# Attention in a hybrid decoder step: logits of two units in a row, DVE's transposition work behind the next maximum, page products on POOL

## The reference

```python
s = jnp.einsum('bqhd,bkhd->bhqk', q_blk, k_all)          # 16 heads of 64
s = s + fq_blk.transpose(0, 2, 1)[..., None] - f_k[:, :, None, :]
s = jnp.where((kpos[None, :] <= qpos[:, None])[None, None], s, -jnp.inf)
p = jax.nn.softmax(s, axis=-1)
return jnp.einsum('bhqk,bkhd->bqhd', p, v_all)
```

## Time and profile before

| what | value |
| --- | --- |
| median of 3 runs | 3183.25 us (3177.59 to 3183.7) |
| the profiled execution | 3182.08 us, of which the span is 3180.5 us |
| busy over the whole span | PE 2896.3 us (91%), DVE 1533.9, ACT 951.6, POOL 751.7 |
| attention phase, roughly 2012 to 2912 us | 28% of the span |
| one middle step of attention (steps 1 to 6; starts of unit 0 at 2160.18, 2267.46, 2374.71, 2481.99, 2590.73, 2697.97 and 2805.26 us) | 107.25 us (one is 108.74) |
| the first step, the last step up to PE's last sum | 110.4 us; 2805.26 to 2904.12 us |

### The profile page before, as it was taken

One profiled execution on the slowest core, in us unless ns is written; L12 is line 12 of the kernel. 1 busy time (PEld: TensorE's weight loads), 2 busy tenths in 40 slices (PEclk: granted clock), 3 DMA queues, 4 the chain that ended last, 5 costly groups with the idle time before them and its releaser, 6 DMA issues. The chain is left out here.

```text
span 3180.5 us, 41505 instructions
## 1 busy us (share of the span) xinstructions
PE 2896.3 (91%) x15730; PEld 2010.4 (63%) x15730; DVE 1533.9 (48%) x3562; ACT 951.6 (30%) x1547; POOL 751.7 (24%) x428
## 2 busy tenths in 40 slices
PE   6589999997899987999969999699999999995998
PEld 2367777776677875777857788344444444442767
DVE  1542222211877637531175115667766776663343
ACT  0322212211655544210042111143434334433000
POOL 1220000000000003000020000376677677676000
PEclk7689999998899998999989999699999999997999
DMA  9532222213466524221142331423322331313764
GB/s 335 186 90 80 54 86 80 77 47 118 158 227 199 160 90 179 82 74 48 47 178 73 77 47 52 127 71 104 104 54 82 104 94 45 101 32 122 249 206 127
DMA packets 281926, 355.19 MB, mean 112 GB/s; under 512 B 40044, under 2 KB 172460, under 8 KB 281681
## 3 DMA queue, kind: packets, MB, share of 16 engines
q1 hardware_dynamic: 279364, 344.23, 34.3%
q0 software_dynamic: 2304, 8.39, 0.7%
q10 hardware_dynamic: 72, 0.07, 0.0%
HBM read 250.28 MB, written 102.10 MB: 111 GB/s over the span
## 5 line engine op out<-in xcount | busy, mean ns | idle before, releaser
L2315 POOL TENSOR_TENSOR at_p_sum<-at_p_sum,at_p 128x1024 f32<-128x1024 f32 (+3 forms) x264 | 543.0, 2057 | 93.2 <-ACT at_p L2171 76.0
L2171 ACT ACTIVATE at_p<-psum 128x1024 f32<-128x1024 f32 (+1 forms) x320 | 286.6, 896 | 504.1 <-PE psum L2011 498.9
L2217 DVE CUSTOM_DVE_ANT_0 psum<-psum,at_f_wide 128x512 f32<-128x512 f32 (+3 forms) x640 | 376.8, 631 | 0.0
L2091 PE MATMUL psum<-at_p,at_v 128*64 128x512 f32 (+3 forms) x1280 | 305.4, 556 | 0.1
L672 POOL TENSOR_TENSOR kv_h_lo<-kv_aux,kv_h_hi 128x512 fp32r<-128x512 f32 x16 | 24.1, 1505 | 1060.2 <-ACT kv_h_hi L649 1023.4
L768 PE MATMUL psum<-kv_w_hi,kv_h_hi 128*128 128x512 f32 x512 | 201.5, 394 | 12.2 <-DVE kv_w_lo L964 12.2
L768 PE MATMUL psum<-gla_w_hi,gla_h_hi 128*128 128x512 f32 x512 | 201.3, 393 | 2.7 <-DVE gla_w_lo L964 2.7
L769 PE MATMUL psum<-kv_w_lo,kv_h_hi 128*128 128x512 f32 x512 | 200.5, 392 | 0.0
L770 PE MATMUL psum<-kv_w_hi,kv_h_lo 128*128 128x512 f32 x512 | 200.2, 391 | 0.0
L769 PE MATMUL psum<-gla_w_lo,gla_h_hi 128*128 128x512 f32 x512 | 199.5, 390 | 0.0
L770 PE MATMUL psum<-gla_w_hi,gla_h_lo 128*128 128x512 f32 x512 | 199.3, 389 | 0.0
(11 more groups left out here) (425 smaller groups left out, 6093.6 us busy)
## 6 DMA issues: line engine op xcount, KB each, us to landing
mod_w<-in_ada_w SPq DMA_DIRECT2D x12, 2048.0 KB, 17.9
at_f_wide<-F SPq DMA_DIRECT2D x32, 512.0 KB, 5.7
at_page<-in_cache_k SPq DMA_DIRECT2D x32, 512.0 KB, 3.9
gla_w_raw<-in_gla_w_in SPq DMA_DIRECT2D x6, 2048.0 KB, 7.8
mod_w<-in_kv_ada_w SPq DMA_DIRECT2D x4, 2048.0 KB, 9.9
v_gla<-gla_stage SPq DMA_DIRECT2D x32, 256.0 KB, 2.0
sg_gla<-gla_stage SPq DMA_DIRECT2D x32, 256.0 KB, 2.0
gl_sg<-sg_gla SPq DMA_DIRECT2D x16, 512.0 KB, 3.9
```

The lines of the kernel that those rows point to most:

```text
L2091: mm = pe.matmul(bank_o[half[a], skip:NB], v[u][:, i, half[a]], p_tile[e % PT][:, a, skip:NB], start=(i == 0), stop=(i == R * G + R - 1), ...
L2171: act.activation(p_tile[e % PT][:, :, skip:NB], pair_of(bank_st[e % 2])[:, :, skip:NB], ACT.Exp)\
L2217: op = dve.tensor_tensor_reduce(pair_of(at(n))[:, a, 0:w], pair_of(at(n))[:, a, 0:w], f_wide[:, a, c * NB:c * NB + w], 1.0, -3.0e38, ALU.s ...
L2315: pool.tensor_tensor(p_sum[s][:, :, skip:NB], p_sum[s][:, :, skip:NB], p_tile[e % PT][:, :, skip:NB], ALU.add).then_inc(p_added, 1)
```

## The change

Five edits, all in the attention phase:

1. PE takes two units together (`two_units`). It waits once for both pairs of banks, makes the masks of both, the maximum of slot e, the logits of e and of e + 1, the maximum of slot e + 1, the turn operation of e, the weighing of units e - 2 and e - 1, and the turn operation of e + 1. ACT does both exponentials first, then the turn work and the copy of `bank_o`.
2. On DVE (`some`), a turn operation of an odd slot comes behind the next slot's maximum; that of an even slot behind the maximum of the slot after it.
3. The slot behind unit 39 is gone. Its m_row is now `CARRIED` into slot 0 of the next step, and the last two weighings of a step lie in unit 0 and 1 of the next.
4. The product of page and query row runs on POOL (`weigh_page`), at the slots 1, 10, 20 and 31, behind that slot's addition. On DVE only the sums remain, each in two halves of 8 heads, at the slots 5, 7, 12, 14, 27, 29, 36 and 38.
5. SP waits for two more maxima before it loads the next V, and loads pages at the new slots.

```diff
-    page_at = (1, 5, 10, 12, 20, 29, 33, 38)
+    page_at = (1, 10, 20, 31)
+    score_at = (5, 7, 12, 14, 27, 29, 36, 38)
...
-                        sp.wait_ge(max_full, UN * (2 * j + u) + AHEAD + 1)
+                        sp.wait_ge(max_full, UN * (2 * j + u) + AHEAD + 3)
...
-                    pe.wait_ge(p_ready, UN * h + e + 1)
+                    pe.wait_ge(p_ready, UN * h + e + 2)
...
+                def two_units(j, u, e):
+
+                    logits_wait(j, u, e)
+                    for s in (e, e + 1):
+                        G, i = exp_units[s]
                         if i >= R * G:
-                            masks(bank_st[e % 2], (i - R * G) * P, g.hide_kq)
...
+                            masks(bank_st[s % 2], (i - R * G) * P, g.hide_kq)
+                    max_unit(j, u, e)
+                    logits(j, u, e)
+                    logits(j, u, e + 1)
+                    max_unit(j, u, e + 1)
+                    turn_unit(j, u, e)
                     if e:
+                        weigh_v(j, u, e - 2)
                         weigh_v(j, u, e - 1)
+                    elif not is_first(j, u):
+                        weigh_v(*previous(j, u), UN - 2)
+                        weigh_v(*previous(j, u), UN - 1)
+                    turn_unit(j, u, e + 1)
...
+                    for e in range(0, UN, 2):
+                        some(e, MAXIMA)
+                        if e:
+                            some(e - 1, TURNS)
+                        some(e + 1, MAXIMA)
+                        some(e, TURNS)
+                        for s in (e, e + 1):
+                            if s in score_at:
+                                score_page(j, u, score_at.index(s))
...
+                    pool.tensor_tensor(page[w % 2][:, :], page[w % 2][:, :], q_sample[u][:, :], ALU.mult).then_inc(page_prod, 1)
...
                     for e in range(UN):
                         add(j, u, e)
+                        if e in page_at:
+                            weigh_page(j, u, page_at.index(e))
```

More of the change, by code:

```diff
@@ L1762, in attention_phase @@
     max_slots = list(enumerate([(OWN, f) for f in last_maxima] + [(NEXT, f) for f in ahead]))
-    turn_slots = {2: (LAST, "sum", 3, 0), 3: (LAST, "pick", 3, 0), 4: (LAST, "spread", 3, 0),
+    turn_slots = {0: (CARRIED, "m_row", 2, 0), 2: (LAST, "sum", 3, 0), 3: (LAST, "pick", 3, 0), 4: (LAST, "spread", 3, 0),
                   6: (OWN, "sum", 0, 0), 7: (OWN, "pick", 0, 0), 8: (OWN, "spread", 0, 0),
@@ L1768, in attention_phase @@
                   26: (OWN, "sum", 2, 0), 27: (OWN, "pick", 2, 0), 28: (OWN, "spread", 2, 0), 30: (NEXT, "m_row", 1, 0),
-                  32: (NEXT, "turn", 3, 0), 35: (NEXT, "turn", 3, 1), UN: (NEXT, "m_row", 2, 0)}
+                  32: (NEXT, "turn", 3, 0), 35: (NEXT, "turn", 3, 1)}
     def slots_with(*whose):
-        slots, n_turn = [[] for _ in range(UN + 1)], 0
+        slots, n_turn = [[] for _ in range(UN)], 0
         for e, (who, (kind, a, b)) in max_slots:
@@ L1778, in slots_with @@
                     slots[e].append((who, "m_max", a // R, 0, 0))
-        for e in range(UN + 1):
+        for e in range(UN):
             if e in turn_slots and turn_slots[e][0] in whose:
@@ L1793, in attention_phase @@
     start_slots, AT_START = slots_with(OWN, NEXT)
-    mid_slots, EACH = slots_with(LAST, OWN, NEXT)
-    end_slots, _ = slots_with(LAST, OWN)
+    mid_slots, EACH = slots_with(LAST, CARRIED, OWN, NEXT)
+    end_slots, _ = slots_with(LAST, CARRIED, OWN)
     tail_slots = [(LAST,) + f[1:4] + (n,) for n, f in enumerate(f for f in turn_slots.values() if f[0] == LAST)]
     AT_END = sum(f[1] in ("sum", "pick", "spread", "m_row") for slot in end_slots for f in slot)
-    page_at = (1, 5, 10, 12, 20, 29, 33, 38)
+    MAXIMA, TURNS = ("max", "m_max"), ("turn", "m_row", "sum", "pick", "spread")
+    assert UN - 1 not in turn_slots
+    page_at = (1, 10, 20, 31)
+    score_at = (5, 7, 12, 14, 27, 29, 36, 38)
     f_slots = (R, 2 * R, 3 * R, 4 * R)
@@ L2149, in _ @@
                 run_steps(step)
+                weigh_v(PAIRS // 2 - 1, 1, UN - 2)
+                weigh_v(PAIRS // 2 - 1, 1, UN - 1)
                 for who, kind, a, b, n in tail_slots:
@@ L2181, in step @@
                 def step(j, u):
-                    for e in range(UN + 1):
-                        if e < UN:
-                            exponential(j, u, e)
+                    for e in range(0, UN, 2):
+                        exponential(j, u, e)
+                        exponential(j, u, e + 1)
                         for who, kind, a, b, n in slots_of(j, u)[e]:
                             filler(*whose(who, j, u), before(j, u), kind, a, b, n)
-                        for G in range(NG):
+                        if e == 0 and not is_first(j, u):
+                            copy_o(*previous(j, u), NG - 1)
+                        for G in range(NG - 1):
                             if units_to(G) == e:
                                 copy_o(j, u, G)
+                        for who, kind, a, b, n in slots_of(j, u)[e + 1]:
+                            filler(*whose(who, j, u), before(j, u), kind, a, b, n)
                 act.sem_inc(p_ready, 2)
@@ L2270, in step, with some @@
                 def step(j, u):
-                    for e in range(UN + 1):
-                        for who, kind, a, b, n in slots_of(j, u)[e]:
-                            turn_op(*whose(who, j, u), before(j, u), kind, a, b, n)
-                        if e in page_at:
-                            score_page(j, u, page_at.index(e))
+                    def some(s, kinds):
+                        for who, kind, a, b, n in slots_of(j, u)[s]:
+                            if kind in kinds:
+                                turn_op(*whose(who, j, u), before(j, u), kind, a, b, n)
+                    for e in range(0, UN, 2):
+                        some(e, MAXIMA)
[6 more added lines that the diff above has]
+                                score_page(j, u, score_at.index(s))
                 dve.sem_inc(turn_used, 1)
```

63 lines of the change are left out of this document (28 added, 35 removed).

## The result

The changed kernel takes **3129.27 us** (median of 4 runs, 3128.80 to 3129.90) where the kernel before takes 3181.42 (4 runs, 3177.59 to 3183.70): a ratio of 0.984, 95% interval 0.9829 to 0.9852, 52 us less. I had said 3155 us with a range from 3134 to 3176. The profiled execution has a span of 3128.0 us against 3180.5.

What follows compares the result with a forecast made beforehand. PE was taken to bound attention. Saving 4.4 - 0.9 = 3.5 us a middle step gave 24.5 over seven steps, plus 1.8 (first) and 0.5 (last): 26.8 off 3182.1, so 3155 us, range 3134 to 3176.

Steps and rivals of the forecast that it cites:

- the saving of a middle step: Attention's middle steps: 4.4 us saved on changes between kinds of PE products, less 0.9 us of added waits, 3.5 us.
- the three signs: Against the forecast: PE idle before plain pairs' second maximum, PE waiting for exponentials at many pairs, exponential waiting for POOL in group 3.
- The first weighing of two: PE's first of two weighings in a row takes 0.91 us, between bounds of 0.853 and 1.01.
- Turn operations: On PE they keep their price: four transposes some 0.55 us on either side of a weighing.
- Masked second maxima: Ten slots' maxima with a mask now stand behind logits: changes of kind return, 0.2 us each, 2.0 us a step lost.
- The waits: PE waiting for DVE in the new order, mainly at four short pairs: 5.3 us a step, 0.9 more than before.
- Turns behind: DVE's turn work moved behind the next maximum: nothing removed on DVE, worth 0 on its own.
- The pages: Page products moved from DVE to POOL: hidden in middle steps, gaining only unit 11's wait, already counted among the waits.
- What is left on DVE: By the port rule, a product on POOL blocks no remaining DVE operation, each having at most one input in SBUF.
- The last step: Groups 0 to 2 save about 3 us, POOL's extra product ends it 2.5 us later: 0.5 us saved.
- the larger gain: Rival: weighings and maxima join without gap and DVE answers sooner, 6.6 us a step, 3134 us; chance 0.14.

Runs made afterwards that it cites:

- the kernel with the old order: The changed kernel, but DVE does each slot's turn work straight behind that slot's maximum, ahead of the next one: 3209.11 us, ratio 1.0094 to the kernel before.
- the kernel without the pages: The changed kernel with the products of page and query row back on DVE at their old slots: 3157.39 us, ratio 0.9919 to the kernel before.
- the kernel with the pages alone: The kernel before, with only the page products moved to POOL and half page sums on DVE: 3165.37 us, ratio 0.9941 to the kernel before.
- The kernel with turns behind alone: The kernel before, units one at a time, with only DVE's turn work moved behind the next slot's maximum: 3252.40 us, ratio 1.0225 to the kernel before.

## Why the prediction was right or wrong

Of the 52.5 us by which the two spans differ, 44.7 lie in attention and 7.8 outside. I forecast 26.8, all in attention. Two terms of the sum failed: the saving of a middle step (3.5 us said, 5.75 measured), and everything outside attention, which I put at nothing without a reason (7.8 measured). With 44.7 alone the sum would give 3137 us, inside the range.

- **The bound: right.** PE sets attention's time before and after, at a granted clock of 1.00 in the middle steps. None of the three signs that I named against the forecast appeared in the middle steps: no wait for the exponential, no exponential held up by POOL, no idle PE before the second maximum of a plain pair.
- **The first weighing of two: mis-sized.** 0.86 us instead of my 0.91, so 1.0 us a step more. I had the right end of the bounds in hand and took the middle. The rule of the Trainium skill ("TensorEngine Tiling (Array Packing)", Key Properties) that I weighed there, a drain on a change of mode only, leaves bare columns, 0.853 as I had worked them out, and this trace agrees with 0.86.
- **Turn operations: mis-sized.** I let them keep their price on either side of a weighing. What counts is what follows: four transposes cost 0.49 us where a mask follows, 0.66 where a maximum does and 0.59 ahead of a weighing; a pick costs 0.47 ahead of a mask and 0.54 otherwise. In the new order most of those behind the weighings have a mask behind them. That is 0.5 us a step.
- **Masked second maxima: right.** 0.43 us from the maximum to the weighing where 0.33 is plain, and 0.32 from the last logits product to the mask where 0.23 is plain.
- **The waits: right in place, too high in size.** The short pairs hold 0.69 to 0.71 us each by the trace, against a forecast of 0.79 to 0.88. Slots 4, 8 and 28 have 0.08 to 0.19 instead of 0.3, and slot 6 0.29 instead of 0.6. Read as I read the earlier trace rows (later than in a pair that isn't waited for), it comes to about 4.4 us a step instead of 5.3, 0.9 less. For the half sum ahead of slot 6 I had taken DVE's delay in full, though part of it fell in PE's weighings.
- **A middle step.** 3.5 + 1.0 + 0.5 + 0.9 makes 5.9 us, and 107.25 to 101.5 is 5.75; the last 0.15 I can't place. Six steps give 36.1 us, 15 more than the 21 forecast. Of these 1.5 is one step of before that took 108.74 us, with the lower clock in unit 12, and this dip doesn't come back after. The first step gives 6.6 instead of 5.3.
- **Turns behind, "0 on its own": wrong as a statement.** With the pairs it is worth 11.6 us a step, shown by the kernel with the old order. My total didn't suffer, since my waits were counted with the new order. But a reader who left this edit out on my word would have had a slower kernel. Of the three parts it is the one that decides the sign.
- **The pages: the place right, the worth too small.** The middle steps hide POOL's products, as forecast; each takes 2.37 us, and the last sum's wait of 8.24 lies over the 6 I named. But I counted only unit 11's wait. In the new order the product would stand ahead of the short pair (2,3)'s maximum. There it costs 2.5 us, and over the step 3.9, which the kernel without the pages shows. The port rule of the Trainium skill ("SBUF — State Buffer", "Who interferes with whom") keeps a DVE operation with at most one input in SBUF clear of POOL, outside the modes that use two ports. The half sums agree with it: they take 674 to 687 ns wherever they fall, though POOL is busy 83.5 of 101.5 us.
- **What is left on DVE: not free of POOL.** I had dropped the exception from that rule and said that a product on POOL blocks nothing on DVE. The copy `at_spread` has one input in SBUF and is held up all the same: 0.43 us alone, 1.27 beside an addition in the kernel with the pages alone, up to 1.9 with the turns in the old order. That it runs in such a mode isn't shown. In the changed kernel's middle steps it takes at most 0.52, since in its new place it falls between two additions or at the end of one; that is luck, I hadn't looked. The other way round POOL gained by the move: its busy time grew by 6.6 us a step and not 9.5, since its additions no longer stand beside DVE's products (543.0 us for 264 of them before, 521.9 after).
- **The last step: half right.** 105.2 us instead of 107.2 between the same marks, 2.1 less where I said 0.5. Groups 0 to 2 save 4.8 us where I said 3, and group 3 loses 2.7. Of the 4.8, 2.5 come with the pages alone: before, PE waited 2.08 us at unit 11 of this step and had a granted clock of 0.50 for a while after it, and I had priced only the 1.45 of a middle step.
- **Outside attention: put at nothing, 7.8 us measured.** 4.7 lie ahead of attention and 3.1 behind it. In the first phase a load of the GLA weights (gla_w_raw) is issued at 175.4 to 176.7 us in the three traces of before and in the kernel with the pages alone, and at 170.4 to 172.9 in all others. From the output phase on it takes 267.1 to 268.0 us before and 263.4 to 265.3 after. The code of these phases is the same. What differs ahead is the granted clock while the last products of the first phase run (103 to 106 us, before and then after):

```profile
103.00:106.00 3.00, 3.00 (x10) 1.64 (x9) 0.48 (x1) 0.00 (x0) 0.00 (x0) 0.50 0.00 0
```

```profile
103.00:106.00 3.00, 2.41 (x12) 1.10 (x10) 1.34 (x4) 0.00 (x0) 0.00 (x0) 1.00 0.03 6
```

It is 0.50 there in the three traces of before and with the pages alone, and 1.00 in the other nine; in the two traces above eight products on line 174 take 1.88 us and 1.06. Until just before, at some 102 us, PE is at the same product within 2 us in both groups. Why the clock falls there in the one group of kernels and not in the other stays open; no experiment here changes it by itself. The kernel with turns behind alone belongs to the faster group, and so does the one with pairs and pages but without turns behind, so no single part of the change brings it.

Of my rivals, the larger gain was nearest (6.6 us a step in it, 5.75 measured), and within attention it would have held. Its 0.14 was too little: of the bounds that I had worked out, the trace of before already spoke for bare columns, since a logits product costs 0.23 behind another one of its kind and a whole 0.1 more behind another kind. I should have read the weighing in the same way.

## What to carry to other kernels

Where one engine is the bound, price its order from start to start, and price the first of a run of like products from bare columns: grouping like work gives that gain in full. Then look, for each pair of operations that hand over to a second engine, at the time between them against that engine's answer; whatever the second engine does between the two (a turn, a page's product) is paid by the first, and whether it may stand there decides the sign. If a third engine can hold up the second one's work, as POOL's additions do DVE's copy, its place must be looked at too. Don't move the weighing everywhere for a wait that exists in four places: in those four it gained 1.3 us a step, everywhere it lost 4.7.

## What the runs showed of the hardware

A PE wait of 1.58 us in attention was followed, in steps 1 to 7 of the kernel without the pages, by the granted clock at 0.50 (1.2 GHz), and cost 1.5 us on top. In step 0 of the same kernel a wait of 2.09 us was not. Nor does every long wait elsewhere do this: the 1.45 us at unit 11 of before were followed by it in one of the six middle steps, and pair (8,9) of the kernel with the old order waits 1.92 us in each step, and takes 7.75 us in some and 9.3 in others. The changed kernel, with no wait over 0.71 us, shows no such dip in its middle steps.

POOL and DVE hold each other up where both work in SBUF: DVE's copy of 128x512 takes 0.43 us alone and 1.91 when it meets an addition of 2.38, and ends 0.28 us after it; an addition takes 3.19 instead of 2.38 beside DVE's product of two tensors. Half sums of one tensor took 674 to 687 ns throughout.

The kernel's phases ahead of attention were not the same in time from one kernel to the next, though their code was: 3 to 6 us by 176 us, with the granted clock at 0.50 in one group and 1.00 in the other from 103 to 106 us. A comparison of spans alone would have put this to the edit; the split at the first logits product shows it.
